# Mixture-of-experts step of a streaming encoder: 64 tokens per block as the stationary operand in two column groups, packed expert weights moving

## The chip, the cores and the metric

The kernel runs on one NeuronCore of a Trainium2 chip. The metric is device time in microseconds (us) per execution. One execution is also recorded by the hardware profiler; its rows are named by engine: PE is TensorE's matrix multiply, PEld its weight load, DVE is VectorE, ACT is ScalarE, POOL is GpSimd, and SP is SyncE, which issues most DMAs.

## What is computed

One inference step of one encoder layer in float32, for 512 prompt frames and 8 streams of 16 frames, 640 tokens of 1024 features in all: a mixer (attention and a recurrence), cross attention, and a mixture of experts. Only the last concerns the change:

```
grp_prob = softmax(x @ w_grp + b_grp);  g_top, g_idx = top_k(grp_prob, 1)
e_logits = (x @ w_rt + b_rt).reshape(N, 4, 8)
in_grp = take_along_axis(e_logits, g_idx)          # 8 experts of the chosen group
e_top, e_idx = top_k(in_grp, 2);  e_w = softmax(e_top) * g_top
# for each of the 32 experts, over the tokens that chose it:
hg  = silu(x @ w_gate[e]) * (x @ w_up[e])          # (1024, 256) each
out += (hg * comb[:, e]) @ w_down[e]               # (256, 1024)
```

Each token has two of 32 experts, so there are 1280 (token, expert) pairs.

## The kernel before

The layer's earlier parts end with the normed tokens in HBM (`h_rows`, a row of 4 KB per token). The router (`route_dve` and its partners) then sorts the pairs by expert into blocks of `CAP` = 80 slots. An expert with more pairs than slots gets a second block. The router writes the expert of each block (`table_u`), the token row of every slot (`token_all`, a column per block) and the row that the slot's result goes to (`pair_all`). Slots without a pair get spare rows. The number of rounds, two blocks each, is read from `table_u` by every engine, which then runs a loop of that length by itself, held together by semaphores:

- **SP** (`moe_sync`) loads a block's weights into one of two slots of `W`: gate, up, down, 1 MB each. Gate waits until PE has ended gate of the block two before, up and down likewise. The load of every odd block also waits for the gather of the block before it.
- **GpSimd** (`moe_pool`) gathers the token rows of the block two ahead by an indirect DMA (line 2069), then scatters this block's result rows to `pair_rows` (line 2082).
- **PE** (`moe_pe`) runs gate and up of block j (line 2110): for each of 2 x 2 pieces of 128 hidden features, eight matmuls with a 128x128 piece of the weights stationary and the transposed tokens, 80 columns, moving. Then it transposes the next block's tokens (`turn`, line 2094, eight 80x128 pieces), waits for the product, and runs down (line 2119): the hidden activations, 80 columns, stationary, 512 columns of `w_down` moving, for two halves of the output. A float32 matmul appears as two records.
- **ACT** (`moe_act`) takes Silu of gate (line 2135) and copies half of the transposes (2128) and of the output (2139). **DVE** (`moe_dve`) multiplies gate and up (2164), copies the other halves (2151, 2169) and cuts the index columns.

After the loop every token's two rows are loaded back, weighted and added, and the final norm follows. Line 915 and line 1703 belong to the attention of the eight streams: there four matmuls with 32 stationary columns each write to four groups of 32 output partitions, one after another in program order.

```
for m, name in enumerate(("gate", "up")):
    w = W[:, k, 2048 * m:2048 * m + 2048].rearrange("p (c f) -> p c f", c=KC)
    for f in range(2):
        for c in range(KC):
            mm = nc.tensor.matmul(bank[2 + m][:, CAP * f:CAP * f + CAP], w[:, c, f * P:(f + 1) * P], xgT[k][:, c, :], ...)
```

Of the kernel before, what the change touches and what calls it, by code (L numbers as in the profile page):

```python
# [16 lines left out]
ALU = mybir.AluOpType  # L17
# [3 lines left out]
P = 128  # L21
D = 1024
# [11 lines left out]
CAP = 80  # L34
# [13 lines left out]
def constant_columns():  # L48
# [32 lines left out]
    cols["iota_cap"] = np.repeat(np.arange(CAP)[None] * 1.0, P, 0)  # L81
    slot = np.arange(CAP)[:, None] + CAP * np.arange(NBLK)[None]
    cols["empty"] = np.zeros((P, NBLK))
    cols["empty"][:CAP] = (NPAIR + 1 + slot % (2 * CAP))
# [124 lines left out]
def build_encoder_step(nc, a):  # L209

    ctx = ExitStack()
    with ctx:
# [1609 lines left out]
        def route_pe(pe):  # L1822
# [32 lines left out]
        def route_dve(dve):  # L1855
# [125 lines left out]
            r_ = slice(0, CAP)  # L1981
            pf, ov, tf, table = pair_f[r_], over_f[r_], token_f[r_], bank[2][r_, 0:NBLK]
# [3 lines left out]
            tt(ov, ov, C("empty")[r_], ALU.mult).then_inc(r_dve.step("e1"), 1)  # L1986
# [3 lines left out]
            nc.vector.tensor_copy(pair_all[r_, 0:NBLK], pf).then_inc(r_dve.step("pu"), 1)  # L1990
# [9 lines left out]
            nc.vector.tensor_copy(token_all[r_, 0:NBLK], tf).then_inc(r_dve.step("token"), 1)  # L2000
# [62 lines left out]
        def moe_pool(pool):  # L2063

            def gather(j, k):
                pool.wait_ge(e_pe["tr1"], e_pe.after(j - 2, "tr1"))
# [8 lines left out]
            with pool.Fori(0, n) as i:  # L2075
                for k in range(2):
                    j = pool.snap(2 * i + k)
                    gather(j + 2, k)
                    pool.wait_ge(e_act["y0"], e_act.after(j, "y0"))
                    pool.wait_ge(e_dve["y1"], e_dve.after(j, "y1"))  # L2080
                    pool.sem_inc(s_go, 1)
                    pool.indirect_dma_start(a["pair_rows"], bass.IndirectOffsetOnAxis(pair_col[k][0:CAP, :], 0), yb[k][0:CAP, :], None)\  # L2082
                        .then_inc(s_rows[k], 16)

        def moe_pe(pe):
# [3 lines left out]
            def turn(j, k, count):  # L2089
                pe.wait_ge(s_xg[k], count)  # L2090
                for g, s, name in ((0, e_act, "x0"), (1, e_dve, "x1")):
                    pe.wait_ge(s[name], s.after(j - 1, name))
                    for c in range(4):
                        mm = nc.tensor.transpose(bank[g][:, c * CAP:(c + 1) * CAP], xg[k][0:CAP, (4 * g + c) * P:(4 * g + c + 1) * P],  # L2094
                                                 ident[0:CAP, 0:CAP])
                    mm.then_inc(e_pe.step(f"tr{g}"), 1)
# [431 lines left out]
```

## Time and profile before

| | |
|---|---|
| runs | 1432.6, 1433.24, 1438.88 us; median 1433.24 |
| span of the profiled execution | 1429.8 us, 3.4 under that median; its device time is not listed apart |
| PE busy | 1250.6 us, 87% |
| PEld, DVE, ACT, POOL busy | 838.9, 435.8, 310.1, 193.1 us |
| DMA | 221.49 MB, mean 155 GB/s |
| stage of the expert loop, first gate matmul to end of the last down | 1020.2 to 1392.3, 372.1 us |

A busy share over the whole span mixes stages with different limits; the page's slices (the span cut in 40) and a table by windows tell which stage is bound by what. The granted clock is TensorE's: 1.00 stands for 2.4 GHz, 0.50 for 1.2 GHz. The DMA share is the summed time of the packets over 16 DMA engines; packets overlap, so it can pass 1.

### The profile page before, as it was taken

To read this page: it belongs to the slowest core of one execution; us is meant where nothing else is said; L and a number is where in the kernel's file an instruction comes from. 1 tells how busy PE (TensorE), PEld (TensorE's weight loads), DVE (VectorE), ACT (ScalarE), POOL (GpSimd) and SP (SyncE) were. 2 spreads that over 40 slices of the span, in tenths; PEclk is the share of its full clock that TensorE was granted. 3 is DMA by queue.
4 is the path that set the end of the run, shared out by engine and by line. 5 is a ranking of instruction groups with operands and counts; after the bars stand their busy time and mean duration, and the time that the engine had idled before them with its cause. 6 is when DMAs were issued, how large, how long until landed. Compare 5 with 4: busy or idle time off the path is not lost.

```text
span 1429.8 us, 18302 instructions
## 1 busy us (share of the span) xinstructions
PE 1250.6 (87%) x7028; PEld 838.9 (59%) x7028; DVE 435.8 (30%) x949; ACT 310.1 (22%) x620; POOL 193.1 (14%) x222
## 2 busy tenths in 40 slices
PE   5999999987788789989999859994599999999990
PEld 3544555446677676654455644442577778777770
DVE  2002223326656564443210313345211111111115
ACT  2000557524223222102000212220011111111111
POOL 1000454301001001001000000031011111111114
PEclk9999999997989999999999979997599999999995
DMA  8111103111211314007460044410799999999966
GB/s 247 59 59 59 42 18 133 60 48 40 94 60 59 117 59 148 0 0 257 151 221 0 1 176 176 177 45 31 241 293 337 334 338 342 329 335 331 339 199 239
DMA packets 143148, 221.49 MB, mean 155 GB/s; under 512 B 18987, under 2 KB 93611, under 8 KB 142974
## 3 DMA queue, kind: packets, MB, share of 16 engines
q1 hardware_dynamic: 134564, 191.20, 40.1%
q0 software_dynamic: 8496, 29.50, 6.1%
q8 instruction: 31, 0.51, 0.1%
q10 hardware_dynamic: 42, 0.17, 0.1%
q14 instruction: 15, 0.12, 0.0%
HBM read 197.87 MB, written 22.97 MB: 154 GB/s over the span
## 4 chain that ended last, share of the span: by engine, by line
PE 72%; issue 15%; DVE 7%; DMA 2%; ACT 2%; POOL 1%; SPq 1%; DVEq 0%; POOLq 0%; ACTq 0%
PE bank L415 17%; PE bank L2110 16%; PE bank L411 14%; PE bank L2119 8%; PE bank L1074 3%; PE bank L2094 1%; PE bank L1614 1%; PE bank L1684 1%; DMA sb_W<-cache_mem_v 1%; PE bank L721 1%; PE bank L1079 1%; PE bank L741 1%; PE bank L357 1%; PE bank L1587 1%; PE bank L406 1%
## 5 line engine op out<-in xcount | busy, mean ns | idle before, releaser
L2110 PEld LDWEIGHTS bank<-sb_act_b,sb_W 128*128 128x128 f32 x2048 | 240.1, 196 | 17.2 <-issue 17.2
L2110 PE MATMUL bank<-sb_act_b,sb_W 128*128 128x80 f32 x2048 | 239.2, 279 | 0.9 <-DVE sb_act_b L2151 0.9
L415 PE MATMUL bank<-sb_W,sb_act_a 128*128 128x512 f32 x480 | 219.1, 603 | 1.7 <-issue 1.0
L411 PE MATMUL bank<-sb_act_a,sb_W 128*128 128x512 f32 (+1 forms) x768 | 213.1, 435 | 1.3 <-DVE sb_act_a L343 1.3
L411 PEld LDWEIGHTS bank<-sb_act_a,sb_W 128*128 128x128 f32 x768 | 116.0, 191 | 92.8 <-issue 90.7
L415 PEld LDWEIGHTS bank<-sb_W,sb_act_a 128*128 128x128 f32 x480 | 88.8, 193 | 101.2 <-issue 99.6
L2119 PE MATMUL bank<-sb_W,sb_act_b 128*80 128x512 f32 x256 | 118.8, 607 | 1.1
L1074 PE MATMUL bank<-sb_x 128*128 128x128 f32 x512 | 68.3, 284 | 9.7 <-DVE sb_x L1463 6.2
L2164 DVE TENSOR_TENSOR sb_act_b<-bank,sb_act_b 128x160 f32<-128x160 f32 x32 | 10.4, 324 | 216.3 <-PE bank L2110 216.3
L2119 PEld LDWEIGHTS bank<-sb_W,sb_act_b 128*80 128x80 f32 x256 | 36.4, 152 | 60.8 <-issue 60.8
L1074 PEld LDWEIGHTS bank<-sb_x 128*128 128x128 f32 x512 | 61.9, 194 | 16.3 <-DVE sb_x L1463 6.5
L2082 POOL DMA_INDIRECT pair_rows<-sb_act_b,sb_attn x32 | 29.6, 926 | 306.1 <-DVE sb_act_b L2169 306.1
L415 PE MATMUL bank<-sb_W 128*128 128x512 f32 x128 | 56.0, 593 | 1.4 <-DVE sb_W L343 1.4
L2169 DVE COPY sb_act_b<-bank 80x512 f32<-80x512 f32 x32 | 22.0, 687 | 100.2 <-PE bank L2119 100.2
L2128 ACT COPY sb_act_b<-bank 128x320 f32<-128x320 f32 x33 | 14.1, 426 | 147.9 <-PE bank L2094 147.9
L440 ACT COPY sb_conv<-bank 128x512 f32<-128x512 f32 x24 | 14.1, 586 | 147.8 <-PE bank L415 123.8
L321 POOL TENSOR_SCALAR sb_small<-sb_small 128x1 f32<-128x1 f32 x17 | 3.9, 232 | 298.7 <-ACT sb_scr L313 298.4
L415 PEld LDWEIGHTS bank<-sb_W 128*128 128x128 f32 x128 | 23.8, 190 | 29.4 <-issue 27.7
L415 PE MATMUL bank<-sb_conv,sb_act_a 128*128 128x512 f32 x80 | 39.4, 603 | 0.0
L2069 POOL DMA_INDIRECT sb_act_a<-h_rows,sb_attn x34 | 30.8, 907 | 57.0 <-DVE sb_attn L2147 47.3
L2135 ACT ACTIVATE sb_act_b<-bank 128x160 f32<-128x160 f32 x32 | 9.7, 304 | 129.6 <-PE bank L2110 129.6
L357 PE MATMUL bank<-sb_const,sb_scr 128*128 128x128 f32 x136 | 19.8, 303 | 19.5 <-DVE sb_scr L336 19.5
(381 smaller groups left out, 1487.9 us busy)
## 6 DMA issues: line engine op xcount, KB each, us to landing
sb_W<-w_gate SPq DMA_DIRECT2D x32, 1024.0 KB
sb_W<-w_up SPq DMA_DIRECT2D x32, 1024.0 KB
sb_W<-w_down SPq DMA_DIRECT2D x32, 1024.0 KB
sb_W<-w_in SPq DMA_DIRECT2D x7, 2048.0 KB, 8.3
sb_W<-cache_diff_k SPq DMA_DIRECT2D x8, 1024.0 KB, 5.2
sb_W<-cache_diff_v SPq DMA_DIRECT2D x8, 1024.0 KB, 7.4
sb_W<-cache_mem_k SPq DMA_DIRECT2D x8, 1024.0 KB, 4.8
sb_W<-cache_mem_v SPq DMA_DIRECT2D x8, 1024.0 KB, 7.0
```

Source lines behind the costliest of these rows:

```text
L357: mm = nc.tensor.transpose(quarters(bank[4 + 2 * (t % 2) + i])[:, c, :], scr[:, t % 2, q * P:(q + 1) * P], ident)
L406: mm = nc.tensor.matmul(out[0:8, 0:cols.stop - cols.start], w_gab[:, c, :], src[:, c, cols], start=c == 0, stop=c == KC - 1)
L411: mm = nc.tensor.matmul(out[:, 0:cols.stop - cols.start], slot(unit)[:, c, m * P:(m + 1) * P], src[:, c, cols], start=c == 0, stop=c == KC ...
L415: mm = nc.tensor.matmul(out[:, :], src[:, c, ja * P:(ja + 1) * P], w, start=c == 0, stop=c == KC - 1)
L721: mm = nc.tensor.matmul(bank[2 + m][:, 0:P * (t + 1)], dq[rows, h, t * P:(t + 1) * P], dk[rows, h, 0:P * (t + 1)], start=True, stop=True)
L741: mm = nc.tensor.matmul(bank[6 + t % 2][:, h * P:(h + 1) * P], aT[q][:, k * P:(k + 1) * P], dv[:, k, h * P:(h + 1) * P], start=k == 0, sto ...
L1074: mm = nc.tensor.matmul(quarters(out)[:, h, :], h4(lhs)[:, h, :], h4(rhs)[:, h, :], start=start, stop=stop)
L2069: pool.indirect_dma_start(xg[k][0:CAP, :], None, a["h_rows"], bass.IndirectOffsetOnAxis(token_col[k][0:CAP, :], 0))\
L2082: pool.indirect_dma_start(a["pair_rows"], bass.IndirectOffsetOnAxis(pair_col[k][0:CAP, :], 0), yb[k][0:CAP, :], None)\
L2110: mm = nc.tensor.matmul(bank[2 + m][:, CAP * f:CAP * f + CAP], w[:, c, f * P:(f + 1) * P], xgT[k][:, c, :], start=c == 0, stop=c == KC - 1)
L2119: mm = nc.tensor.matmul(bank[4 + g][0:CAP, :], hT[k][:, f, :], w[:, f, 512 * g:512 * g + 512], start=f == 0, stop=f == 1)
L2169: nc.vector.tensor_copy(yb[k][0:CAP, 512:1024], bank[5][0:CAP, :]).then_inc(e_dve.step("y1"), 1)
```

## The change

Blocks hold 64 tokens. The tokens are now the stationary operand of gate and up: for each of eight pieces of the 1024 input features the 64 token columns are loaded twice, for output partitions 0 to 63 and 64 to 127, and 256 weight columns move against each, the first 128 of them gate, the others up. The two output halves hold hidden features 0 to 127 and 128 to 255. Down works likewise: 64 tokens stationary, 512 weight columns moving, output features 0 to 511 in the lower 64 partitions and 512 to 1023 in the upper. Since the hidden activations now lie with tokens on partitions, a PE transpose and a DVE copy (`ht`, `hT`) come between the product and down. A token row is gathered and scattered in two half rows of 2 KB, one to partition t and one to partition 64 + t, so the transposes are four of 128x128. The weights of an expert are packed, before the launch, into one array `w_experts` whose row for a partition holds gate and up (16 KB) and down (8 KB); they come by two DMAs, each with its own semaphore. ACT alone copies the output.

```diff
-CAP = 80
+CAP = 64
...
-            tt(at_place, C("iota_cap").unsqueeze(1).to_broadcast([P, 2 * NT, CAP]), place.unsqueeze(2).to_broadcast([P, 2 * NT, CAP]),
+            tt(at_place, C("iota_cap").unsqueeze(1).to_broadcast([P, 2 * NT, P]), place.unsqueeze(2).to_broadcast([P, 2 * NT, P]),
                ALU.is_equal).then_inc(r_dve.step("ap"), 1)
...
-            nc.vector.tensor_copy(token_all[r_, 0:NBLK], tf).then_inc(r_dve.step("token"), 1)
+            ts(token_all[:, 0:NBLK], tf, 2.0, C("half"), ALU.mult, ALU.add).then_inc(r_dve.step("token"), 1)
...
-                for m, (name, step) in enumerate((("w_gate", "gate"), ("w_up", "up"))):
-                    sp.wait_ge(e_pe[step], e_pe.after(j - 2, step))
-                    sp.dma_start(w[:, 2048 * m:2048 * m + 2048].rearrange("p (c f) -> p c f", c=KC),
-                                 a[name][0][bass.ds(e, 1)].rearrange("o (c p) f -> p (o c) f", p=P)).then_inc(s_ew[k], 16)
-                sp.wait_ge(e_pe["d1"], e_pe.after(j - 2, "d1"))
-                sp.dma_start(w[:, 4096:6144].rearrange("p (f d) -> p f d", f=2),
-                             a["w_down"][0][bass.ds(e, 1)].rearrange("o (f p) d -> p (o f) d", p=P)).then_inc(s_ew[k], 16)
+                src = a["w_experts"][bass.ds(e, 1)].rearrange("o p n -> (o p) n")
+                sp.wait_ge(e_pe["gu"], e_pe.after(j - 2, "gu"))
+                sp.dma_start(W[:, k, 0:4096], src[:, 0:4096]).then_inc(s_eg[k], 16)
+                sp.wait_ge(e_pe["d"], e_pe.after(j - 2, "d"))
+                sp.dma_start(W[:, k, 4096:6144], src[:, 4096:6144]).then_inc(s_ed[k], 16)
...
-                pool.indirect_dma_start(xg[k][0:CAP, :], None, a["h_rows"], bass.IndirectOffsetOnAxis(token_col[k][0:CAP, :], 0))\
+                pool.indirect_dma_start(xg[k], None, h_halves, bass.IndirectOffsetOnAxis(token_col[k], 0))\
                     .then_inc(s_xg[k], 16)
...
-                    for m, name in enumerate(("gate", "up")):
-                        w = W[:, k, 2048 * m:2048 * m + 2048].rearrange("p (c f) -> p c f", c=KC)
-                        for f in range(2):
-                            for c in range(KC):
-                                mm = nc.tensor.matmul(bank[2 + m][:, CAP * f:CAP * f + CAP], w[:, c, f * P:(f + 1) * P], xgT[k][:, c, :],
-                                                      start=c == 0, stop=c == KC - 1)
-                        mm.then_inc(e_pe.step(name), 1)
+                    pe.wait_ge(s_eg[k], i * 16 + 16)
+                    for c in range(KC):
+                        for g in range(2):
+                            mm = nc.tensor.matmul(bank[2][64 * g:64 * g + 64, 0:256], xgT[k][:, c % 4, 64 * (c // 4):64 * (c // 4) + 64],
+                                                  w_gu(k)[:, c, g, :], start=c == 0, stop=c == KC - 1, skip_group_check=True)
+                    mm.then_inc(e_pe.step("gu"), 1)
                     turn(j + 1, 1 - k, i * 16 + 16 + 16 * k)
                     pe.wait_ge(e_dve["h"], e_dve.after(j, "h"))
...
+                    nc.tensor.transpose(bank[1][:, 0:P], hid[k], ident).then_inc(e_pe.step("ht"), 1)
+                    pe.wait_ge(e_dve["hT"], e_dve.after(j, "hT"))
+                    pe.wait_ge(s_ed[k], i * 16 + 16)
+                    pe.wait_ge(e_act["y"], e_act.after(j - 1, "y"))
+                    for f in range(2):
+                        for g in range(2):
+                            mm = nc.tensor.matmul(bank[4][64 * g:64 * g + 64, :], hT[k][:, f, :], w_dn(k)[:, f, 512 * g:512 * g + 512],
+                                                  start=f == 0, stop=f == 1, skip_group_check=True)
+                    mm.then_inc(e_pe.step("d"), 1)
```

On PE, one block of the loop before, from the transposes of the next block's tokens to gate and up of that block (`moe_act`, `moe_dve` are the steps of ACT and DVE, `expert_loaded` the weights):

```order
L2094 MATMUL bank<-sb_const,sb_act_a 128x80 [waits moe_act,tokens_gathered1]
L2094 MATMUL bank<-sb_const,sb_act_a 128x80 x3
L2094 MATMUL bank<-sb_const,sb_act_a 128x80 [waits moe_dve]
L2117 ISA [waits moe_dve2]
L2119 MATMUL bank<-sb_W,sb_act_b 80x512 [waits moe_act1]
L2119 MATMUL bank<-sb_W,sb_act_b 80x512
L2110 MATMUL bank<-sb_act_b,sb_W 128x80 [waits moe_dve2,expert_loaded1,moe_dve,moe_act]
L2110 MATMUL bank<-sb_act_b,sb_W 128x80 x31
```

The same stretch in the changed kernel:

```order
L2100 MATMUL bank<-sb_const,sb_act_a 128x128 [waits moe_dve,moe_act,tokens_gathered1]
L2100 MATMUL bank<-sb_const,sb_act_a 128x128 x3
L2118 MATMUL bank<-sb_const,sb_act_b 128x128 [waits moe_dve2]
L2121 ISA [waits expert_down_loaded0,moe_dve2]
L2124 MATMUL bank<-sb_W,sb_act_b 64x512 [waits moe_act1]
L2124 MATMUL bank<-sb_W,sb_act_b 64x512 x3
L2113 MATMUL bank<-sb_W,sb_act_b 64x256 [waits moe_dve2,expert_gate_up_loaded1,moe_dve,moe_act]
L2113 MATMUL bank<-sb_W,sb_act_b 64x256 x15
```

Between the token transposes and down stands a further transpose (line 2118) that waits for DVE, and a second wait for DVE and for the down weights behind it; gate and up are 16 matmuls, not 32.

On SP, the loads of an odd block before (`moe_pe1` are PE's steps):

```order
L2047 ISA [waits tokens_gathered0]
L2048 ISA [waits moe_pe1]
L2048 DMA sb_W<-w_gate 128x8x256
L2048 DMA sb_W<-w_up 128x8x256 [waits moe_pe1]
L2051 DMA sb_W<-w_down 128x2x1024 [waits moe_pe1]
```

And in the changed kernel:

```order
L2055 ISA [waits tokens_gathered0]
L2056 ISA [waits moe_pe1]
L2056 DMA sb_W<-w_experts 128x4096
L2058 ISA [waits moe_pe1]
L2058 DMA sb_W<-w_experts 128x2048
```

Two loads with two waits on PE stand where three stood; the wait for the gather keeps its place ahead of them.

## Rows read from the trace of the kernel before

**Rows 1.** The page's 40 slices: PE and DMA busy share in tenths.
```profile
PE   5999999987788789989999859994599999999990
DMA  8111103111211314007460044410799999999966
```
**Rows 2.** The page's costliest groups: busy us, mean ns of one | idle before.
```profile
L2110 PE MATMUL bank<-sb_act_b,sb_W 128*128 128x80 f32 x2048 | 239.2, 279 | 0.9 <-DVE sb_act_b L2151 0.9
L2119 PE MATMUL bank<-sb_W,sb_act_b 128*80 128x512 f32 x256 | 118.8, 607 | 1.1
L2164 DVE TENSOR_TENSOR sb_act_b<-bank,sb_act_b 128x160 f32<-128x160 f32 x32 | 10.4, 324 | 216.3 <-PE bank L2110 216.3
```
**Rows 3.** Timeline, start and end of the expert loop: start us, us, what.
```profile
1018.08 0.37 SPq L2048 DMA_DIRECT2D sb_W<-w_gate  x1
1020.16 13.94 PE L2110 MATMUL bank<-sb_act_b,sb_W 128*128 128x80 f32 x64 [0.88 <-DVE sb_act_b L2151]
...
1388.64 3.66 PE L2119 MATMUL bank<-sb_W,sb_act_b 128*80 128x512 f32 x8
```
**Rows 4.** Windows: us, PE, PEld, DVE, ACT, POOL busy, PEclk, DMA share, GB/s.
```profile
1020.20:1392.30 372.10, 371.04 (x2560) 294.36 (x2560) 51.16 (x159) 61.55 (x112) 57.62 (x63) 0.98 0.98 317
1200.00:1360.00 160.00, 159.52 (x1132) 126.65 (x1132) 22.77 (x71) 27.35 (x49) 25.79 (x29) 1.00 1.04 334
1020.20:1038.70 18.50, 18.50 (x77) 16.05 (x78) 0.93 (x4) 1.05 (x4) 0.90 (x1) 0.50 0.90 292
```
**Rows 5.** Timeline of one block of the loop and the next.
```profile
1206.30 0.72 PE L2094 MATMUL bank<-sb_const,sb_act_a 80*128 80x80 f32 x8
1207.04 3.65 PE L2119 MATMUL bank<-sb_W,sb_act_b 128*80 128x512 f32 x8
1210.54 7.27 PE L2110 MATMUL bank<-sb_act_b,sb_W 128*128 128x80 f32 x64
1214.27 0.30 ACT L2135 ACTIVATE sb_act_b<-bank 128x160 f32<-128x160 f32 x1 [3.29 <-PE bank L2110]
1217.94 0.33 DVE L2164 TENSOR_TENSOR sb_act_b<-bank,sb_act_b 128x160 f32<-128x160 f32 x1 [6.52 <-PE bank L2110]
1221.89 7.27 PE L2110 MATMUL bank<-sb_act_b,sb_W 128*128 128x80 f32 x64
```
**Rows 6.** Windows as in rows 4: rows of 1 KB, of 4 KB, twice mostly 11 KB.
```profile
1211.30:1212.00 0.70, 0.70 (x9) 0.70 (x8) 0.12 (x1) 0.00 (x0) 0.00 (x0) 1.00 1.10 350
1214.80:1215.50 0.70, 0.70 (x8) 0.70 (x8) 0.00 (x0) 0.00 (x0) 0.00 (x0) 1.00 1.07 421
24.00:26.00 2.00, 2.00 (x6) 0.80 (x6) 0.00 (x0) 0.00 (x0) 0.00 (x0) 1.00 1.11 441
26.00:28.00 2.00, 2.00 (x6) 0.92 (x5) 0.00 (x0) 0.00 (x0) 0.00 (x0) 1.00 0.98 407
```
**Rows 7.** Timeline: matmuls that go to four column groups in turn.
```profile
862.66 1.07 PE L1703 MATMUL bank<-sb_W,sb_attn 128*32 128x256 f32 x16
342.29 1.06 PE L915 MATMUL bank<-sb_act_b,sb_W 128*32 128x512 f32 x8
```
**Rows 8.** Timeline: a transpose, a routing operation.
```profile
864.63 0.38 PE L1709 MATMUL bank<-sb_const,sb_attn 128*128 128x128 f32 x2
1004.78 0.99 DVE L1978 TENSOR_TENSOR sb_attn<-sb_const,sb_attn 128x800 f32<-128x800 f32 x1
```
**Rows 9.** DMA queues from 1050 to 1200: packets, MB, share of 16 engines.
```profile
q0 software_dynamic: 2496, 8.52, 17.2%
```
**Rows 10.** DMA issues: count, KB each, median us to landing.
```profile
sb_W<-w_cq SPq DMA_DIRECT2D x2, 2048.0 KB, 7.7
sb_act_a<-h_rows,sb_attn POOLq DMA_INDIRECT x34, 6.9
```
**Rows 11.** Windows as in rows 4: two stretches with PE partly idle.
```profile
318.60:339.00 20.40, 11.12 (x46) 8.93 (x47) 11.65 (x30) 12.18 (x17) 3.10 (x2) 0.50 0.24 87
431.20:444.80 13.60, 8.48 (x71) 7.77 (x71) 7.85 (x17) 3.27 (x8) 2.61 (x2) 1.00 0.42 155
```

More of the change, by code:

```diff
@@ L80, in constant_columns @@
     cols["slot0"] = np.repeat(CAP * np.arange(NBLK)[None] * 1.0, P, 0)
[L81 to L84, printed above, removed]
+    cols["iota_cap"] = np.repeat((np.arange(P) % CAP)[None] * 1.0, P, 0)
+    slot = (np.arange(P) % CAP)[:, None] + CAP * np.arange(NBLK)[None]
+    cols["empty"] = NPAIR + 1 + slot % (2 * CAP)
+    cols["half"] = (p >= CAP) * 1.0
     return {k: np.asarray(v, np.float32) for k, v in cols.items()}
@@ L2090, in turn @@
                 pe.wait_ge(s_xg[k], count)
[L2091 to L2096, printed above, removed]
+                pe.wait_ge(e_act["x0"], e_act.after(j - 1, "x0"))
+                pe.wait_ge(e_dve["x1"], e_dve.after(j - 1, "x1"))
+                for c in range(4):
+                    mm = nc.tensor.transpose(quarters(bank[3 * (c // 2)])[:, c % 2, :], xg[k][:, c * P:(c + 1) * P], ident)
+                mm.then_inc(e_pe.step("x"), 1)
             turn(0, 0, 16)
@@ L2116, in moe_pe @@
-                    for g, s, name in ((0, e_act, "y0"), (1, e_dve, "y1")):
-                        pe.wait_ge(s[name], s.after(j - 1, name))
-                        for f in range(2):
-                            mm = nc.tensor.matmul(bank[4 + g][0:CAP, :], hT[k][:, f, :], w[:, f, 512 * g:512 * g + 512], start=f == 0, stop=f == 1)
-                        mm.then_inc(e_pe.step(f"d{g}"), 1)
+                    nc.tensor.transpose(bank[1][:, 0:P], hid[k], ident).then_inc(e_pe.step("ht"), 1)
+                    pe.wait_ge(e_dve["hT"], e_dve.after(j, "hT"))
@@ L2126, in turned @@
             def turned(j, k):
-                act.wait_ge(e_pe["tr0"], e_pe.after(j, "tr0"))
-                nc.scalar.copy(xgT[k][:, 0:4, :], bank[0][:, 0:4 * CAP].rearrange("p (c s) -> p c s", c=4)).then_inc(e_act.step("x0"), 1)
+                act.wait_ge(e_pe["x"], e_pe.after(j, "x"))
+                nc.scalar.copy(xgT[k][:, 0:2, :], quarters(bank[0])[:, 0:2, :]).then_inc(e_act.step("x0"), 1)
             turned(0, 0)
@@ L2133, in moe_act @@
                     j = act.snap(2 * i + k)
-                    act.wait_ge(e_pe["gate"], e_pe.after(j, "gate"))
-                    nc.scalar.activation(sgate[k], bank[2][:, 0:2 * CAP], ACT.Silu).then_inc(e_act.step("silu"), 1)
+                    act.wait_ge(e_pe["gu"], e_pe.after(j, "gu"))
+                    nc.scalar.activation(sgate[k], bank[2][:, 0:P], ACT.Silu).then_inc(e_act.step("silu"), 1)
                     turned(j + 1, 1 - k)
-                    act.wait_ge(e_pe["d0"], e_pe.after(j, "d0"))
+                    act.wait_ge(e_pe["d"], e_pe.after(j, "d"))
                     act.wait_ge(s_rows[k], i * 16 + H_ROWS[k])
-                    nc.scalar.copy(yb[k][0:CAP, 0:512], bank[4][0:CAP, :]).then_inc(e_act.step("y0"), 1)
+                    nc.scalar.copy(yb[k], bank[4][:, :]).then_inc(e_act.step("y"), 1)
         def moe_dve(dve):
@@ L2143, in moe_dve @@
             n = rounds(dve)
[L2144 removed]
             def columns(j, k):
[L2147 removed]
+                nc.vector.tensor_copy(token_col[k], token_all[:, bass.ds(j, 1)]).then_inc(e_dve.step("ix"), 1)
             def turned(j, k, j2):
[L2150 to L2151 removed]
+                dve.wait_ge(e_pe["x"], e_pe.after(j, "x"))
+                nc.vector.tensor_copy(xgT[k][:, 2:4, :], quarters(bank[3])[:, 0:2, :]).then_inc(e_dve.step("x1"), 1)
                 columns(j2, k)
@@ L2517 @@
     arrays["const"] = _np.concatenate([CONST[k] for k in CONST_AT], axis=1)
+    gate, up, down = (arrays.pop(n)[0] for n in ("w_gate", "w_up", "w_down"))
+    gate_up = _np.stack([w.reshape(NE, KC, P, 2, P) for w in (gate, up)], axis=4)
+    arrays["w_experts"] = _np.ascontiguousarray(_np.concatenate(
+        [gate_up.transpose(0, 2, 1, 3, 4, 5).reshape(NE, P, 4096),
+         down.reshape(NE, 2, P, D).transpose(0, 2, 1, 3).reshape(NE, P, 2048)], axis=2))
     aps = {}
```

71 lines of the change are left out of this document (35 added, 36 removed).

## The prediction

> **What bounds the kernel now.** I read the page's slices first: in the last third of the span TensorE (PE) and the DMA engines both stand at 9 for nine slices running, and in no other slice do both [rows 1]. The costliest groups say whose time that is: line 2110 (gate and up) and line 2119 (down), the expert loop [rows 2]. It runs from the first gate matmul at 1020.2 to the end of the last down step at 1392.3, 372.1 us [rows 3, 4].
>
> The timeline of one block shows its rhythm [rows 5]: 7.27 us of gate and up, 0.72 us of transposes, 3.65 us of down, and the next block starts 11.35 us after the last (1210.54 to 1221.89). PE is busy 159.5 of 160 us, so **PE is the bound**. But the DMA share beside it is 1.04 [rows 4]. The stage is bound twice, nearly to the same degree, and a change to PE alone would be worth little.
>
> Why each is slow: there are 64 records of gate and up a block (2048 over 32), 7.27/64 = 0.114 us each, and the eight down records of 512 columns take 3.65 with some 0.22 for start and end, so 0.43 each. A moving column therefore costs 0.43/512 = 0.83 ns, and the 80 columns of a gate record 0.067 us. The other 0.047 is spent since every such record brings 128 new columns of weights: the gate and up matmuls go at the pace of weight loads. On the DMA side the 1 KB rows of gate and up run at 350 GB/s, the 4 KB rows of down at 421 [rows 6].
>
> **The change, part by part.**
>
> *Gate and up on PE.* 16 matmuls (32 records) move 256 weight columns each, 0.213 us a record by the column price. They alternate between two column groups. Whether two groups run side by side decides everything, and the trace shows it: line 1703 sends 16 records of 256 columns to four groups of 32 in 1.07 us, line 915 8 records of 512 columns in 1.06 [rows 7]. One after another they would take 3.4 and 3.4. Four abreast, 4 x 0.213 + 0.22 and 2 x 0.427 + 0.2 fit both. I take two abreast as full overlap: 16 x 0.213 + 0.22 = **3.6 us** a block, against 7.27. The weight loads (64 columns, half of what costs 0.11) stay under the 0.213 of a slot.
>
> *Down.* 8 records of 512 columns, two abreast: 4 x 0.427 + 0.2 = **1.9**, against 3.65.
>
> *The new hops.* Before, eight transposes covered Silu and the product; now four transposes do, and behind the product come a PE transpose (ht), a DVE copy and only then down. Silu 0.30, less for 128 columns [rows 5]; the product 0.33 for 160 columns, so 0.3 for 128, and the copy the same; a transpose 0.38 [rows 8]; each handover near 0.1 (gate and up end at 1217.81, the product starts at 1217.94). Sum 0.3 + 0.3 + 0.4 + 0.3 + 5 x 0.1 = **1.8**, on the path. PE chain of a block: 3.6 + 1.8 + 1.9 = **7.3 us**, against 11.35.
>
> *DMA.* Per block three loads of 1 MB become two of 2 and 1 MB with rows of 16 and 8 KB, 3.146 MB as before; the tokens go from 80 rows of 4 KB each way to 128 half rows of 2 KB, 0.66 to 0.52 MB. No transfer of before has rows so long in this stage. Bounds: the rate of the 1 KB rows now, 350 GB/s, gives (3.146 + 0.524)/0.350 = 10.5 us; the best window, in which the constants come in rows of 11 KB, 441 [rows 6], gives 8.3. Nearest are those long rows, 441 and 407 in two windows, and the down rows at 421 [rows 6]; by 422, 3.146/0.422 = 7.5. The token queue takes 17.2% of 150 us for 8.52 MB [rows 9], that is 330 GB/s, so 0.524 MB cost 1.6. Together **9.1 us** a block. That exceeds 7.3, so the bound moves from PE to the DMA queue, and PE will wait for weights 1.8 us a block. The Trainium skill, "DMA: Bandwidth & Descriptors", Specifications, puts one core's share of HBM near 358 GB/s; by that a block would take 10.3 us, an estimate. Windows at 441 and 421 stand against it as a ceiling here.
>
> *What could starve the queue.* Gate-and-up weights for block j+2 are requested when gate and up of j end, down weights when down of j ends, 3.6 and 7.3 us after j's weights land; their turn in the queue comes 9 and 14 us later. GpSimd issues the gather for j+3 behind the scatter of j, about 11 us after j's weights land; it lands 7 us later [rows 10], at 18, and is wanted at 2 x 9.1 + 3.6 = 22. That leaves 4 us; it is what would be late next.
>
> *More blocks.* A block holds 64 tokens, not 80. The trace doesn't show the loads per expert; the reference's router on its inputs gives 22 to 71 pairs for the 32 experts, two of them over 64. So 34 blocks, 17 rounds; now 32 (the product of line 2164 has 32 instances [rows 2]).
>
> *Routing before the loop.* Tables of 54 columns become 58, one DVE operation grows from 800 to 1280 elements, at 0.99 us for 800 [rows 8] some 0.5 more; the 20 records of the table matmul load 128 columns, not 80, at the half clock, 1.7 us at most; with smaller ones and longer gathers **+3 us**, all ahead of the first gate matmul. Packing the weights is done outside the kernel and costs nothing here.
>
> **The sum.** The first gate matmul starts at 1020.2 + 3 = 1023.2. The clock there is half [rows 4], so gate and up of block 0 take 16 x 0.427 + 0.22 = 7.0, to 1030.2. Block 1's weights are asked for behind the first gather [rows 3], so 3 later, at 1021.1; a 2 MB load into a quiet queue lands in 7.7 [rows 10], so 1028.8. Block 2's are asked for at 1030.2 and land at 1038.8 with tokens between; block 3's follow gate and up of block 1, which begin when block 0 is done (1036) and end between 1039.6 and 1043, so they land near 1048.5. From there the queue sets the pace: 30 more at 9.1 bring block 33's weights to 1321.5, and its chain of 7.3 ends at **1328.8**. Before it ended at 1392.3. Saved: **63.5 us**. What follows is unchanged. The profiled span is 1429.8; the median of the runs, 1433.24, is 3.4 above, which I take as what lies around the span and leave. 1433.2 - 63.5 = 1369.7, forecast **1370**.
>
> **The rivals.**
> - *The clock falls, sometimes.* PE now waits between blocks. With PE 55% busy the trace has the granted clock at 0.50 (1.2 GHz) for 20 us; with 62% it stayed at 1.00 [rows 11]. Here the hops leave PE idle for about 1.2 of their 1.8, so it will be busy 6.1 of 9.1, 67%. The Trainium skill, "TensorE: Matmul & The Clock Gate", HAM oscillation, tells of matmuls that wait for DMA each round and then run at half clock, which speaks against this change. One block at 1.2 GHz costs 7.0 + 2.0 + 3.7 = 12.7 us, but then PE waits for no weights, as in the loop of before, which held 1.00. If 55% of the work ran so: 7.3 + 0.55 x 5.4 = 10.3 a block, 34 x 10.3 = 350, the loop's end at 1373 in place of 1392, about 1414.
> - *The clock stays at 1.2 GHz*, as in the 18.5 us at the loop's start, PE full and the clock 0.50 [rows 4]. 34 x 12.7 = 432, with the 3 before it 63 more than 372: **1496, slower**. It decides from a mean block of (372 - 3)/34 = 10.9 us on, that is once half of the blocks run so and the rest at 9.1. Against: PE was just as full then, with records that brought new weights for 80 columns each, and the low stretch ended in the first down step, whose records move 512 columns; mine move 256 and 512.
> - *The column groups don't overlap* (the change doesn't do what it says): 6.8 + 0.2 + 1.8 + 3.6 = 12.4 a block, 34 x 12.4 = 422, 1486, slower. Against it stand the two runs of four groups [rows 7].
> - *Long rows bring nothing*: 10.5 a block, 30 x 1.4 later, 1412. The 10.3 from the Trainium skill's Specifications above would come to 1406.
>
> **How the numbers follow.** Forecast 0.63; clock falls at times 0.14; long rows bring nothing 0.12; clock stays low 0.07; no overlap 0.02; the last 0.02 for a late gather that eats the gain. Queue rates of 441 and 350 move 30 blocks by -24 and +42 us: 1346 and 1412. I give 1344 to 1415, which takes in the two milder rivals. A difference of 0.5% (7 us) is about what a measurement of this kernel tells from none: faster 0.88, same 0.03, slower 0.09.
>
> **What would show it.** Right: the loop's blocks 9 to 9.4 us apart, 34 of them; line 2113 in about 3.6 us a block and 2124 in 1.9; PE idle ended by the weight DMA; rates above 390 GB/s. Wrong: a granted clock under 1 in the loop, 2113 at 7 us, PE waiting for a gather, or rates still near 350.

## The result, and the profile after

The changed kernel takes 1359.7 us (median of 4 runs, 1353.4 to 1360.26) beside 1435.18 us for the kernel before (4 runs, 1432.6 to 1438.88). The ratio is 0.9463, 95% interval 0.9432 to 0.9495: 75 us faster, where the forecast had 63.5. The profiled execution took 1360.26 us with a span of 1358.4, so 1.9 us lie around the span.

The slices come first again: PE, DMA and the rate of the changed kernel.

```profile
PE   5999999996888778999899987799826777777760
...
DMA  9211013101113111500736101542128999999975
GB/s 260 63 62 62 1 62 140 63 0 67 63 63 124 62 62 62 155 0 0 270 125 208 60 1 36 225 180 117 78 93 317 425 423 423 425 424 424 425 323 236
```

Where both rows stood at 9 before [rows 1], PE now stands at 7 and only the DMA engines at 9, at a rate that stays between 423 and 425 GB/s for seven slices. The page's costliest groups, with busy us and mean ns of one ahead of the idle time before them and what ended most of it, tell whose idle time that is:

```profile
L2113 PE MATMUL bank<-sb_W,sb_act_b 128*64 128x256 f32 x1088 | 127.2, 387 | 48.4 <-DMA sb_W<-w_experts 47.6
...
L2124 PE MATMUL bank<-sb_W,sb_act_b 128*64 128x512 f32 x272 | 65.9, 604 | 15.7 <-DVE sb_act_b L2170 15.7
```

Gate and up had 0.9 us of idle time ahead of them in the whole loop [rows 2], and none of it was put down to weights; now they have 48.4, and 47.6 of it ends with a weight DMA. The timeline shows the loop's first steps, one block in its middle, and its end (start us, us, what):

```profile
1028.32 5.96 PE L2113 MATMUL bank<-sb_W,sb_act_b 128*64 128x256 f32 x32 [0.81 <-DVE sb_act_b L2156]
...
1053.97 3.67 PE L2113 MATMUL bank<-sb_W,sb_act_b 128*64 128x256 f32 x32 [0.64 <-DMA sb_W<-w_experts]
...
1201.21 3.67 PE L2113 MATMUL bank<-sb_W,sb_act_b 128*64 128x256 f32 x32 [1.48 <-DMA sb_W<-w_experts]
...
1204.81 0.66 PE L2100 MATMUL bank<-sb_const,sb_act_a 128*128 128x128 f32 x4
1204.93 0.28 ACT L2141 ACTIVATE sb_act_b<-bank 128x128 f32<-128x128 f32 x1 [3.20 <-PE bank L2113]
...
1205.23 0.29 DVE L2168 TENSOR_TENSOR sb_act_b<-bank,sb_act_b 128x128 f32<-128x128 f32 x1 [7.13 <-ACT sb_act_b L2141]
...
1205.58 0.33 PE L2118 MATMUL bank<-sb_const,sb_act_b 128*128 128x128 f32 x1
1205.95 0.29 DVE L2170 COPY sb_act_b<-bank 128x128 f32<-128x128 f32 x1 [0.42 <-PE bank L2118]
...
1206.37 1.94 PE L2124 MATMUL bank<-sb_W,sb_act_b 128*64 128x512 f32 x8 [0.46 <-DVE sb_act_b L2170]
...
1209.95 3.67 PE L2113 MATMUL bank<-sb_W,sb_act_b 128*64 128x256 f32 x32 [1.65 <-DMA sb_W<-w_experts]
...
1313.91 3.67 PE L2113 MATMUL bank<-sb_W,sb_act_b 128*64 128x256 f32 x32 [1.65 <-DMA sb_W<-w_experts]
1319.07 1.94 PE L2124 MATMUL bank<-sb_W,sb_act_b 128*64 128x512 f32 x8 [0.46 <-DVE sb_act_b L2170]
```

Read it from the block at 1201.21: 3.67 us of gate and up, the new hops from Silu at 1204.93 to the copy's end, 1.94 of down, and then a wait for weights. The fourth block starts at 1053.97 and the last, the 34th, at 1313.91: 259.94 us for 30 blocks, **8.66 us a block** (11.35 before [rows 5]). The loop lasts from 1028.32 to 1321.01, 292.7 us, against 372.1. Two windows of the loop (columns as in rows 4), the second one without its start:

```profile
1028.30:1033.00 4.70, 4.68 (x22) 2.68 (x24) 0.00 (x0) 0.92 (x1) 0.94 (x1) 0.50 0.92 384
...
1060.00:1300.00 240.00, 180.69 (x1253) 96.66 (x1249) 27.91 (x135) 51.88 (x96) 54.82 (x56) 1.00 1.01 424
```

PE is busy 75% of the time and the granted clock is 1.00 (2.4 GHz) all the same, behind a low start of 4.7 us, where before it took 18.5 [rows 4]. The waits of this window give the size of the hole that the DMA leaves in PE's time (us in total, times, longest), and the DMA queues from 1100 to 1250 say where the transfer time goes (packets, MB, share of 16 engines):

```profile
PE bank L2113 <- DMA sb_W<-w_experts: 43.9, 28, 1.8
```

```profile
q1 hardware_dynamic: 4974, 54.45, 86.1%
q0 software_dynamic: 2763, 9.09, 15.0%
```

The account of the span: 1429.8 - 1358.4 = 71.4 us saved (the medians differ by 75.5; the runs of before lie up to 6.3 apart). The loop gives 372.1 - 292.7 = 79.4; it begins 8.2 later than before (1028.3 against 1020.2); what follows it takes 37.4 in place of 37.5.

### The profile page after: what moved, and what is told of

Read it like the earlier page. It is cut to its first block, busy times and chain, and to the rows that moved or that the text cites. A ratio compares the mean times of both kernels' runs of the same rounds, so it can differ in the third digit from the quotient of the medians.

```text
span 1358.4 us, 16294 instructions
## 1 busy us (share of the span) xinstructions
PE 1110.7 (82%) x5994; PEld 668.1 (49%) x5994; DVE 420.0 (31%) x959; ACT 311.1 (23%) x627; POOL 201.5 (15%) x226
## 4 chain that ended last, share of the span: by engine, by line
PE 54%; DMA 18%; issue 16%; DVE 7%; ACT 2%; POOL 1%; SPq 1%; DVEq 0%; POOLq 0%; ACTq 0%
PE bank L415 18%; DMA sb_W<-w_experts 16%; PE bank L411 15%; PE bank L2113 5%; PE bank L1074 3%; PE bank L1614 1%; PE bank L1684 1%; DMA sb_W<-cache_mem_v 1%; PE bank L721 1%; PE bank L741 1%; PE bank L357 1%; PE bank L1819 1%; PE bank L1079 1%; PE bank L1587 1%; PE bank L406 1%
## 5 line engine op out<-in xcount | busy, mean ns | idle before, releaser
L2113 PE MATMUL bank<-sb_W,sb_act_b 128*64 128x256 f32 x1088 | 127.2, 387 | 48.4 <-DMA sb_W<-w_experts 47.6
L2113 PEld LDWEIGHTS bank<-sb_W,sb_act_b 128*64 128x64 f32 x1088 | 83.3, 139 | 106.1 <-issue 42.9
L2168 DVE TENSOR_TENSOR sb_act_b<-bank,sb_act_b 128x128 f32<-128x128 f32 x34 | 9.9, 291 | 240.2 <-ACT sb_act_b L2141 240.2
L2124 PE MATMUL bank<-sb_W,sb_act_b 128*64 128x512 f32 x272 | 65.9, 604 | 15.7 <-DVE sb_act_b L2170 15.7
L2088 POOL DMA_INDIRECT pair_rows<-sb_act_b,sb_attn x34 | 33.6, 988 | 218.2 <-ACT sb_act_b L2145 218.2
L440 ACT COPY sb_conv<-bank 128x512 f32<-128x512 f32 x24 | 14.1, 586 | 149.5 <-PE bank L415 123.8
L2075 POOL DMA_INDIRECT sb_act_a<-h_rows,sb_attn x36 | 35.0, 972 | 61.0 <-DVE sb_attn L2152 50.6
L2145 ACT COPY sb_act_b<-bank 128x512 f32<-128x512 f32 x34 | 19.9, 585 | 86.3 <-PE bank L2124 86.3
L2141 ACT ACTIVATE sb_act_b<-bank 128x128 f32<-128x128 f32 x34 | 9.4, 277 | 131.0 <-PE bank L2113 131.0
L2124 PEld LDWEIGHTS bank<-sb_W,sb_act_b 128*64 128x64 f32 x272 | 17.0, 136 | 41.1 <-issue 41.1
L651 ACT ACTIVATE sb_scr<-sb_conv,sb_convw 128x664 f32<-128x664 f32 x48 | 36.7, 840 | 0.0
## 6 DMA issues: line engine op xcount, KB each, us to landing
sb_W<-w_experts SPq DMA_DIRECT2D x34, 1024.0 KB, 12.9
```

The lines of the kernel that those rows point to most:

```text
L440: ins = nc.scalar.mul(o, b, scale) if scale != 1.0 else nc.scalar.copy(o, b)
L651: nc.scalar.mul(taps[:, j, :], cv[:, m, j:j + NY], convw[:, m, j:j + 1]).then_inc(c_mul.step(f"m{j}"), 1)
L2075: pool.indirect_dma_start(xg[k], None, h_halves, bass.IndirectOffsetOnAxis(token_col[k], 0))\
L2088: pool.indirect_dma_start(pair_halves, bass.IndirectOffsetOnAxis(pair_col[k], 0), yb[k], None)\
L2113: mm = nc.tensor.matmul(bank[2][64 * g:64 * g + 64, 0:256], xgT[k][:, c % 4, 64 * (c // 4):64 * (c // 4) + 64], w_gu(k)[:, c, g, :], start ...
L2124: mm = nc.tensor.matmul(bank[4][64 * g:64 * g + 64, :], hT[k][:, f, :], w_dn(k)[:, f, 512 * g:512 * g + 512], start=f == 0, stop=f == 1, s ...
```

## The experiments

The theory after the result: before, PE at the pace of weight loads was the bound and DMA stood close behind; the change nearly halves PE's matmul time by two column groups side by side, and the long rows lift the DMA rate from the 350 GB/s of 1 KB rows to 424; now the pace is bytes over that rate. The rivals: it is all the long rows; it is all PE; the pace now is set by the chain of hops or by the gathers; the clock has a share in it.

### Long rows alone

The kernel before, with the weights packed so that each of its three loads has rows of 8 KB. PE's work stays.

```diff
-                for m, (name, step) in enumerate((("w_gate", "gate"), ("w_up", "up"))):
+                src = a["w_experts"][bass.ds(e, 1)].rearrange("o p n -> (o p) n")
+                for m, step in enumerate(("gate", "up", "d1")):
                     sp.wait_ge(e_pe[step], e_pe.after(j - 2, step))
-                    sp.dma_start(w[:, 2048 * m:2048 * m + 2048].rearrange("p (c f) -> p c f", c=KC), ...)
+                    sp.dma_start(w[:, 2048 * m:2048 * m + 2048], src[:, 2048 * m:2048 * m + 2048]).then_inc(s_ew[k], 16)
...
-                sp.dma_start(w[:, 4096:6144].rearrange("p (f d) -> p f d", f=2), ...)
```

> The kernel before with the packed weights alone: three loads of 1 MB with rows of 8 KB per block, PE's work as before. Theory (PE bounds the loop before, weights are in time): the blocks stay 11.35 us apart and the time within 4 us of before, 1431 to 1439. Rival (the DMA share of 1.04 meant that DMA bounded it as well): blocks nearer to (3.15 + 0.66) MB / 424 GB/s = 9.0 us, the time 1360 to 1380.

Measured: 1433.64 us (1430.85 to 1439.71, 12 runs) beside 1433.91, ratio 0.9995, 0.9981 to 1.0009. The timeline of PE and a window (columns as in rows 4):

```profile
1158.68 7.27 PE L2107 MATMUL bank<-sb_act_b,sb_W 128*128 128x80 f32 x64
```

```profile
1100.00:1250.00 150.00, 149.54 (x1050) 117.80 (x1049) 21.37 (x66) 26.59 (x47) 23.70 (x26) 1.00 0.96 336
```

PE is busy 149.5 of 150 us, as it was, and the DMA share fell from 1.04 [rows 4] to 0.96 at the same rate. Quicker transfers bring nothing while PE is the bound: the kernel before was PE's. The DMA queues from 1100 to 1250:

```profile
q1 hardware_dynamic: 5740, 41.79, 78.4%
q0 software_dynamic: 2507, 8.53, 17.4%
```

The share of 0.96 at 336 GB/s did not mean a full queue: the changed kernel moves 424 at 1.01. By these lines the 8 KB rows ran at 355 GB/s, not at the 422 of the changed kernel's weights. Shares and rates read while PE is the bound were poor prices, as the run with one column group shows below.

### The new matmuls on short rows

The changed kernel, with its weights laid out so that gate and up come in rows of 1 KB and down in rows of 4 KB, as before.

```diff
-                sp.dma_start(W[:, k, 0:4096], src[:, 0:4096]).then_inc(s_eg[k], 16)
+                sp.dma_start(W[:, k, 0:4096].rearrange("p (c n) -> p c n", c=2 * KC),
+                             a["w_gate_up"][bass.ds(e, 1)].rearrange("o c p n -> p (o c) n")).then_inc(s_eg[k], 16)
...
-                sp.dma_start(W[:, k, 4096:6144], src[:, 4096:6144]).then_inc(s_ed[k], 16)
+                sp.dma_start(W[:, k, 4096:6144].rearrange("p (f d) -> p f d", f=2),
+                             a["w_down_rows"][bass.ds(e, 1)].rearrange("o (f p) d -> p (o f) d", p=P)).then_inc(s_ed[k], 16)
```

> The changed kernel with rows of 1 KB for gate and up and 4 KB for down, as before; PE's work as changed. Theory (the loop is now bound by the DMA queue, whose rate hangs on the row length): gate and up at 350 GB/s take 6.0 us in place of 4.9, so blocks 9.7 to 9.9 us apart in place of 8.66, 34 to 42 us more, 1394 to 1402. Rival (bytes alone set the pace, PE's share was the whole gain): 8.7 us apart, within 5 us of 1360.

Measured: 1394.83 us (1392.11 to 1397.75, 4 runs), ratio to the kernel before 0.9724, 0.9698 to 0.9749. Two blocks on PE, and the window:

```profile
1160.63 3.67 PE L2114 MATMUL bank<-sb_W,sb_act_b 128*64 128x256 f32 x32 [2.63 <-DMA sb_W<-w_gate_up]
...
1170.55 3.67 PE L2114 MATMUL bank<-sb_W,sb_act_b 128*64 128x256 f32 x32 [2.82 <-DMA sb_W<-w_gate_up]
```

```profile
1100.00:1250.00 150.00, 108.42 (x683) 57.18 (x685) 15.53 (x75) 28.59 (x53) 31.14 (x32) 0.93 1.07 373
```

The DMA queues from 1100 to 1250:

```profile
q1 hardware_dynamic: 35728, 48.12, 93.1%
q0 software_dynamic: 2400, 7.87, 13.6%
```

Blocks are 9.7 and 9.9 us apart in turn, 9.82 on average from the fourth to the last, and PE waits 2.6 to 2.8 us for weights in each, at 373 GB/s; the weights' queue went at 345, not 422. So of 75 us the new matmuls, with the smaller blocks and half rows, bring 39 by themselves, the long rows 0 by themselves, and the two together 75: row length is worth 35 us, but only once PE is out of the way.

### Both column groups in one

The changed kernel with all of its matmuls writing to output partitions 0 to 63, so that the two groups can't run side by side. The upper half of the hidden features and of the output is left out of what follows.

```diff
-                            mm = nc.tensor.matmul(bank[2][64 * g:64 * g + 64, 0:256], ...
+                            mm = nc.tensor.matmul(bank[2][0:64, 256 * g:256 * g + 256], ...
...
-                            mm = nc.tensor.matmul(bank[4][64 * g:64 * g + 64, :], ...
+                            mm = nc.tensor.matmul(bank[4 + g][0:64, :], ...
```

> The changed kernel with both halves of gate and up, and of down, written to the lower 64 partitions, so that all records use one column group; the upper half of the hidden features and of the output is left out of what follows. Theory (two groups run side by side, one does not): gate and up 32 x 0.213 + 0.2 = 7.0 us, down 3.6, blocks 12.2 to 12.5 us apart, about 34 x 3.7 = 125 us more, 1480 to 1490, PE the bound again. Rival (the gain on PE came from fewer weight columns, not from side by side): gate and up near 3.7 us and the time within 10 us of 1360.

Measured: 1480.27 us (one run). The timeline of a block:

```profile
1152.09 7.07 PE L2113 MATMUL bank<-sb_W,sb_act_b 128*64 128x256 f32 x32
...
1160.64 3.64 PE L2124 MATMUL bank<-sb_W,sb_act_b 128*64 128x512 f32 x8 [0.46 <-DVE sb_act_b L2170]
```

The same records with the same operands take 7.07 and 3.64 us in one group, 3.67 and 1.94 in two. The overlap is whole, to within the 0.2 or so at start and end, and it is what decides this change: without it the kernel would be some 46 us slower than before. The DMA queues from 1100 to 1250:

```profile
q1 hardware_dynamic: 3582, 39.81, 71.3%
q0 software_dynamic: 1920, 6.29, 11.9%
```

These are the transfers of the changed kernel with PE as the bound. By the same reading they ran at 372 and 352 GB/s, where the changed kernel's had 422 and 404.

### Weights for the first two blocks alone

The changed kernel without the loads of all later rounds; each block computes with the weights of the first round, so that nothing waits for weights.

```diff
-            n = rounds(sp)
-            with sp.Fori(1, n) as i:
-                for k in range(2):
-                    load(i, k)
...
-                    pe.wait_ge(s_eg[k], i * 16 + 16)
+                    pe.wait_ge(s_eg[k], 16)
...
-                    pe.wait_ge(s_ed[k], i * 16 + 16)
+                    pe.wait_ge(s_ed[k], 16)
```

> The changed kernel that loads weights for the first round alone; all later blocks compute with the weights of these two experts. Theory (PE's chain without weight waits is what the second and third block showed, 7.0 us from 1037.54 to 1044.56, and the clock stays at 1.00): blocks 7.0 us apart, 34 x 1.66 = 55 us less, near 1305. Rival (the token chain, gather behind scatter, comes next and holds blocks at 8 us or more): 1330 or above, with PE waiting for the gather.

Measured: 1305.39 us (one run). Two blocks on PE:

```profile
1155.88 3.63 PE L2109 MATMUL bank<-sb_W,sb_act_b 128*64 128x256 f32 x32
...
1162.76 3.63 PE L2109 MATMUL bank<-sb_W,sb_act_b 128*64 128x256 f32 x32
```

That is PE's chain with its hops: 6.88 us a block, 1.8 under the changed kernel's 8.66. The hops do not set its pace. For the gathers this run says less, since they land in 3.4 us here, with no weights beside them, and in 8.9 in the changed kernel; but there, from 1060 to 1300, none of PE's waits is for a gather.

### One and two megabytes more per block

The changed kernel with one more load per block, into a buffer that nobody reads in the loop: 2048 columns (1.05 MB) in one kernel, 4000 (2.05 MB) in the other.

```diff
+            def more(k, e):
+                src = a["w_experts"][bass.ds(e, 1)].rearrange("o p n -> (o p) n")
+                sp.dma_start(conv[:, 2048 * k:2048 * k + 2048], src[:, 0:2048]).then_inc(s_more[k], 16)
...
+                if not isinstance(i, int):
+                    sp.wait_ge(s_more[k], i * 16)
+                    more(k, e)
...
+            for k in range(2):
+                more(k, 0)
```

> The changed kernel with one more load of 1 MB per block from the second round on, into a buffer that nothing reads. Theory (pace by bytes; PE has slack, so a fall of its clock costs nothing): (3.67 + 1.05) MB / 424 GB/s = 11.1 us a block, 32 x 2.5 = 79 us more, 1437 to 1443, with the granted clock under 1 in part of the loop. Rival (with 4 us of waiting a block the clock falls to 1.2 GHz and stays, and PE's chain of 12.7 us becomes the bound): 12.5 us or more a block, 1485 to 1497.

> The same with 2.05 MB more (16000 bytes per partition). Theory (bytes): 13.5 us a block, 32 x 4.8 = 155 us more, 1512 to 1520, wherever the clock stands, since even PE's chain at 1.2 GHz (12.7) is shorter. Rival (the queue loses rate when more is waiting in it): more than 1525.

Measured: 1441.47 and 1516.92 us (one run each). The window of the loop with 1.05 MB more, and two of its blocks on PE:

```profile
1060.00:1300.00 240.00, 161.45 (x975) 85.53 (x977) 21.73 (x105) 40.04 (x74) 43.07 (x44) 0.89 1.01 423
```

```profile
1161.26 3.67 PE L2123 MATMUL bank<-sb_W,sb_act_b 128*64 128x256 f32 x32 [1.35 <-DMA sb_W<-w_experts]
...
1172.32 5.36 PE L2123 MATMUL bank<-sb_W,sb_act_b 128*64 128x256 f32 x32 [3.96 <-DMA sb_W<-w_experts]
```

And with 2.05 MB more:

```profile
1060.00:1300.00 240.00, 153.62 (x812) 78.90 (x810) 18.55 (x90) 33.77 (x63) 35.24 (x36) 0.82 1.01 425
```

The rate stays where it was, 423 and 425 GB/s. The 34 loads carry 35.7 and 69.6 MB, by 424 GB/s 84 and 164 us; the kernels took 81.8 and 157.2 longer than the change. All but a few per cent of the added bytes are paid at that rate, so **the loop is bound by bytes**. The clock did fall here: after a wait of 3.96 us gate and up took 5.36 us, not 3.67. It cost nothing that shows: the total is that of the bytes.

### Empty slots not moved

If bytes are the price, 896 of the 34 x 64 slots carry no pair and are gathered and scattered for nothing. Here their row number lies past the end of the table, and the indirect DMA leaves such rows out.

```diff
-            ts(ov, pf, float(NPAIR), -float(NT * P), ALU.is_ge, ALU.mult).then_inc(r_dve.step("p3"), 1)
+            ts(ov, pf, float(NPAIR), 0.0, ALU.is_ge, ALU.mult).then_inc(r_dve.step("p3"), 1)
...
-                pool.indirect_dma_start(xg[k], None, h_halves, bass.IndirectOffsetOnAxis(token_col[k], 0))\
+                pool.indirect_dma_start(xg[k], None, h_halves, bass.IndirectOffsetOnAxis(token_col[k], 0), bounds_check=2 * NT * P - 1, oob_is_err=False)\
...
-                    pool.indirect_dma_start(pair_halves, bass.IndirectOffsetOnAxis(pair_col[k], 0), yb[k], None)\
+                    pool.indirect_dma_start(pair_halves, bass.IndirectOffsetOnAxis(pair_col[k], 0), yb[k], None, bounds_check=2 * NPAIR - 1, oob_is_err=False)\
```

> The changed kernel in which the gather and the scatter skip the slots that hold no pair (an index bound, instead of reading and writing spare rows). 34 blocks have 2176 slots for 1280 pairs, so 896 x 4 KB fall away each way, 7.3 MB. Theory (the queue moves bytes at 424 GB/s and nothing else binds): 7.3 MB / 424 GB/s = 17 us less, blocks 8.1 to 8.2 us apart, 1340 to 1345. Rival (a skipped row still costs its place in the queue, or GpSimd's work per gather grows with the test): within 4 us of 1360.

Measured: 1350.86 us (1348.01 to 1352.71, 6 runs), ratio to the kernel before 0.9416, 0.9389 to 0.9444. 9 us of the 17 came, a time outside both ranges that had been written down. The window, the token queue, and the first gate and last down matmuls of the loop:

```profile
1100.00:1250.00 150.00, 117.39 (x810) 62.58 (x810) 18.61 (x90) 33.42 (x63) 36.61 (x36) 1.00 1.01 414
```

```profile
q0 software_dynamic: 2873, 5.29, 9.3%
```

```profile
1025.20 5.97 PE L2113 MATMUL bank<-sb_W,sb_act_b 128*64 128x256 f32 x32 [0.81 <-DVE sb_act_b L2156]
...
1309.81 1.94 PE L2124 MATMUL bank<-sb_W,sb_act_b 128*64 128x512 f32 x8 [0.46 <-DVE sb_act_b L2170]
```

The bytes did go, from 9.09 to 5.29 MB in 150 us; the rate fell with them, from 424 to 414. The loop itself took 286.6 us, 6 less than the 292.7 of the changed kernel; the rest of the 9 lies around it. Two explanations: leaving a row out costs time of its own, or the DMA engines are no longer loaded alike. For the second: slots are filled from partition 0 up, so that the low partitions are nearly always used. Suppose that partitions are dealt to engines in groups of four, so that an engine serves two groups of one half's 64 partitions. Then the router's counts for these inputs load the busiest engine with 214 of its 272 slots, and it saves 21%, not 41%, of the 42 us that token rows cost (34 x 0.524 MB at 424 GB/s): 9 us, an estimate. With eight neighbouring partitions to an engine the busiest would save next to nothing. The Trainium skill, "DMA: Bandwidth & Descriptors", The descriptor swizzle, gives the dealing in groups of four for a transfer to 128 partitions. No row of the profile names the engine of a packet.

### Empty slots spread over the groups

The kernel above with the slots of a block dealt round the partition groups in turn. It leaves out the same number of rows.

```diff
-    cols["iota_cap"] = np.repeat((np.arange(P) % CAP)[None] * 1.0, P, 0)
+    q = np.arange(P) % CAP
+    turn, group = q % 4 + 4 * (q // 32), q % 32 // 4
+    cols["iota_cap"] = np.repeat((8 * turn + np.where(turn % 2, 7 - group, group))[None] * 1.0, P, 0)
```

> As the run that skips empty slots, but slot s of a block no longer lies on partition s: eight slots in turn go to partitions 0, 4, 8 ... 28, the next eight back again to their neighbours, and so on through both halves of 32. Theory: skipping gave 9 us and not 17 since a DMA engine serves fixed partitions (four in each run of 32), the low slots are always filled, and the engine with most filled slots sets the pace; from the block sizes the fullest share holds 214 of 272 slots, so 21% of 34 x 0.524 MB / 424 GB/s = 42 us was saved, 9 us. Spread, the fullest holds 163 of 272: 40%, 17 us less than the changed kernel, 1341 to 1346. Rival (the skipped rows cost something in themselves, placement has no part): within 3 us of the run that skips without spreading, 1348 to 1354.

Measured: 1340.98 us (1336.22 to 1345.73, 5 runs) beside 1436.38 (9 runs), ratio 0.9334, 0.9307 to 0.936. The window:

```profile
1100.00:1250.00 150.00, 119.84 (x822) 63.60 (x824) 19.00 (x93) 34.39 (x64) 36.65 (x36) 1.00 1.01 421
```

```profile
1029.45 5.96 PE L2115 MATMUL bank<-sb_W,sb_act_b 128*64 128x256 f32 x32 [0.81 <-DVE sb_act_b L2158]
...
1303.50 1.94 PE L2126 MATMUL bank<-sb_W,sb_act_b 128*64 128x512 f32 x8 [0.46 <-DVE sb_act_b L2172]
```

The rate is back at 421 GB/s, 19 us of the 42 are saved, and the loop takes 276.0 us, 16.7 less than in the changed kernel. The busiest engine would have 163 of 272 slots now, by which 40% or 17 us were due. What held the last kernel back was where its rows lie, not that others were left out. That it is the load of the engines is an inference. The totals fit it, 9 and 19 us for 9 and 17, the loops less closely, 6 and 17; by the ratios to the kernel before, the savings are 7 and 18.5 with some 6 to either side (an estimate from the intervals). And the mean DMA share is 1.01 in both windows, where engines short of work should have lowered it in the first; but a share was no measure of spare room in the run with long rows alone either. This is the fastest kernel of the study, 6.7% under the kernel before, 1.4% under the change.

**Not tried.** Two experts get a second block, and their weights are loaded twice, 7.4 us each by 3.146 MB at 424 GB/s. A third slot for weights could fill ahead of the loop, where the page's slice has the DMA engines busy two tenths.

## Why the prediction came out right, and what was off

The direction, the mechanism and the range held. Point by point:

- **The bound moves from PE to the DMA queue**: shown. Long rows alone brought nothing, added bytes are paid in full, and with the loads gone a block takes 6.88 us. The wait forecast at 1.8 us a block is 43.9/28 = 1.6.
- **Gate and up 3.6, down 1.9, full overlap**: 3.67 and 1.94; shown by the kernel with one column group. The rival without overlap had forecast 1486; that kernel took 1480.27.
- **Hops 1.8**: from gate and up's end near 1204.88 to down at 1206.37, 1.5. PE chain 7.3: 6.88 without waits.
- **DMA 9.1 us a block: the step that was mis-sized.** Measured 8.66, under the 9 to 9.4 that was to be the sign of it. Its weights term was right: queue q1 moved 54.45 MB in 86.1% of 150 us, 422 GB/s, which makes 7.5 us for 3.146 MB. That was in part luck. The windows behind it last 0.7 and 2 us; the one of 0.7 us with 421 lies in a stretch, from 1214 to 1216.2, that had 376 and in which token rows moved too, and the 8 KB rows of the run with long rows alone had 355. The token term was wrong. I priced 0.524 MB at the 330 GB/s of the token queue before, 1.6 us; q0 above has 9.09 MB in 15.0% of 150 us, 404 GB/s, 1.3 us. The runs say where that comes from. With PE as the bound, and long weight rows in both, 80 rows of 4 KB had 327 and 128 half rows 352; with the queue as the bound the half rows had 386 beside short weight rows and 404 beside long ones. So the smaller part belongs to the tokens' new transfers, and the larger to reading a rate while PE was the bound; why such rates are low is open. The two terms make 8.76, and the last 0.1 comes off since packets overlap (the shares add to 1.01). 30 blocks x (9.1 - 8.66) = 13 us, and the loop was forecast at 1328.8 - 1023.2 = 305.6 against 292.7 measured: the pace explains the whole of that miss, and the token rate some 9 us of it.
- **34 blocks**: line 2113 has 1088 records, 34 x 32.
- **Gather with 4 us to spare**: of the waits from 1060 to 1300 none has PE waiting for a gather, though it took 8.9 us to land, not 7. SP held the loads of odd blocks back for it, 27.8 us in 14 times, and the DMA share stayed at 1.01 all the same. In the loop's third block PE did wait 1.93 us for one, ahead of the transposes; it waited 0.64 for weights right after, so that cost nothing.
- **Routing +3 us**: the comparison grew from 0.99 to 1.49 us and the table matmul from 2.92 to 4.52, 2.1 for the two, as forecast. In the kernel before, and then in the changed one:

```profile
993.07 0.43 DVE L1931 TENSOR_TENSOR sb_attn<-sb_attn,sb_const 128x256 f32<-128x256 f32 x1
...
1006.46 2.92 PE L1841 MATMUL bank<-sb_attn 128*80 128x54 f32 x20 [14.09 <-DVE sb_attn L1980]
```

```profile
999.32 0.49 DVE L1931 TENSOR_TENSOR sb_attn<-sb_attn,sb_const 128x320 f32<-128x320 f32 x1
...
1011.63 1.49 DVE L1978 TENSOR_TENSOR sb_attn<-sb_const,sb_attn 128x1280 f32<-128x1280 f32 x1
...
1013.86 4.52 PE L1841 MATMUL bank<-sb_attn 128*128 128x58 f32 x20 [15.22 <-DVE sb_attn L1980]
```

  But the first gate matmul came 8.2 later, not 3. Line 1931, the first operation that the change widens, already starts 6.25 late, so that the routing itself cost 1.9. With the routing of before the loop started at 1020.2 and, in the run with long rows alone, at 1025.8; the change and its seven variants above started it between 1023.0 and 1029.7. So the 5 us by which the start was missed lie within the scatter from run to run. What makes that scatter stays open.
- **Around the span** I left 3.4 us; it is 1.9. That, the start and the pace add up to the difference: 1369.7 + 5.1 - 12.9 - 1.5 = 1360.4, the profiled execution's 1360.26. The late start and the quick pace pull opposite ways, so that the total came 5 us nearer to the forecast than the loop did: that is luck.
- **The clock rivals** didn't come: 1.00 through the loop, low for 4.7 us at its start. PE's busy share would not have settled it beforehand: 67% was reckoned with and 75% came, but in the kernel with 1.05 MB more PE was busy 161.45 of 240 us, 67%, and the granted clock was 0.89. A lower clock there only fills time in which PE would wait.
- **Long rows bring nothing** (10.5 us a block, 1412) fell: with the rows of before under the new matmuls the kernel takes 1394.83, 35 us more than with long ones. With it fell the remark that a change to PE alone would be worth little: with the old rows it brought 39 us. The 10.5 us priced all bytes at the rate of 1 KB rows, though a third of the weights comes in rows of 4 KB; the blocks were 9.82 us apart. The 10.3 us worked out from the Trainium skill's "DMA: Bandwidth & Descriptors", Specifications, fell with it: 424 GB/s over 240 us stand against 358. The Trainium skill, "DMA: Bandwidth & Descriptors", Bandwidth, says that its own higher figures are for one core of a pair with the other idle. This kernel runs on one core.

## What to carry to other kernels

Where a stage is bound by two things to nearly the same degree, price both after the change: half of it was worth 0 us and the other half 39, together they were worth 75. A rate read from rows of another length, or while something else is the bound, is a bound and no price: the same weights and tokens showed 372 and 352 GB/s with PE as the bound, 422 and 404 with the queue as the bound. And once bytes are the bound, look for bytes that carry nothing, and then at how evenly what is left lies over the partitions.

## What had not been expected of the hardware

- Two column groups of 64 with 256 moving columns overlap fully: 7.07 us in one group, 3.67 in two, for the same 32 records.
- Token half rows of 2 KB ran at 404 GB/s in their queue, beside 16 and 8 KB weight rows at 422; the 4 KB token rows before had 330 [rows 9]. Half as long was no worse, and the lower rates go with a queue that is not the bound: the half rows had 352 with PE as the bound, and 334 with no weights moving (11.27 MB in 22.5% of 150 us).
- PE at 75% with holes of 1.5 to 1.65 us in each block kept 2.4 GHz; with holes of 2.6 to 2.8 us (1 KB rows) the granted clock was 0.93, with added bytes 0.89 and 0.82. None of that cost time, since PE still waited for weights in these loops.
- Rows left out of gathers and scatters saved 9 us with the slots in order and 19 with them spread over the partitions (6 and 17 within the loop), for the same number of rows.
